# D times x on GpSimd in the chunk loop of a state-space stage, and finished chunks turned one step later

## The reference, cut to what matters

```
x = silu(conv(xbc)); xs, bm, cm = split(x)            # xs: 8 heads of 64
y_f, fin_f = ssd_chunked(xs, dt_f, a_f, bm, cm, init_f)
y_b, fin_b = ssd_chunked(flip(xs), flip(dt_b), a_b, flip(bm), flip(cm), init_b)
y = y_f + flip(y_b) + d_skip[:, None] * xs
y = y * silu(z)
out = rms_norm(y, g_out)
```

## Time and profile before

| | us |
|---|---|
| median of 3 runs | 1674.86 (1671.91 to 1675.18) |
| the profiled execution | 1675.81 |
| its span, first to last instruction | 1673.9 |
| TensorE busy | 1625.1 (97%) |
| VectorE busy | 1018.1 (61%) |
| ScalarE busy | 705.4 (42%) |
| GpSimd busy | 101.5 (6%) |

### The profile page before, as it was taken

The page is one execution under the profiler, slowest core; times in us unless marked ns, Lnnn a source line. Parts: engine busy times, 40 slices in busy tenths (PEclk is TensorE's granted clock), DMA queues, the critical chain, the costliest instruction groups (busy, mean ns, idle before and its releaser), DMA issues. The chain is left out here.

```text
span 1673.9 us, 25018 instructions
## 1 busy us (share of the span) xinstructions
PE 1625.1 (97%) x9735; PEld 1416.4 (85%) x9735; DVE 1018.1 (61%) x1689; ACT 705.4 (42%) x1288; POOL 101.5 (6%) x123
## 2 busy tenths in 40 slices
PE   6999999999899999999999999999999999999997
PEld 4787888877688889878889999999999998888886
DVE  3653645258754555555587666656665665477787
ACT  4632112357554544545664333333333334434453
POOL 1101000013000000321000000000000000000011
PEclk9999999999999999999999999999999999999999
DMA  9323441013300000323312222212222226763445
GB/s 370 148 98 144 155 157 52 1 49 102 83 11 10 14 1 2 107 88 132 126 51 79 90 81 106 106 73 90 90 95 82 100 81 216 231 219 98 124 162 191
DMA packets 76293, 176.36 MB, mean 105 GB/s; under 512 B 10352, under 2 KB 26944, under 8 KB 74128
## 3 DMA queue, kind: packets, MB, share of 16 engines
q1 hardware_dynamic: 72080, 169.75, 29.1%
q0 software_dynamic: 4096, 5.01, 0.9%
HBM read 131.02 MB, written 43.70 MB: 104 GB/s over the span
## 5 line engine op out<-in xcount | busy, mean ns | idle before, releaser
L374 PE MATMUL psF<-gv,gu_ring 128*128 128x384 f32 (+1 forms) x664 | 220.7, 332 | 3.9 <-DVE gv L2745 3.2
L375 PE MATMUL psF<-gv,gu_ring 128*128 128x384 f32 (+1 forms) x664 | 220.1, 332 | 0.0
L376 PE MATMUL psF<-gv,gu_ring 128*128 128x384 f32 (+1 forms) x664 | 220.0, 331 | 0.0
L381 PE MATMUL psF<-gv,gu_ring 128*128 128x512 f32 x540 | 193.6, 392 | 0.0
L382 PE MATMUL psF<-gv,gu_ring 128*128 128x256 f32 x540 | 151.3, 280 | 0.0
L374 PE MATMUL psF<-d_w_ring,d_hid_ring 128*128 128x512 f32 x360 | 140.2, 389 | 0.0
L375 PE MATMUL psF<-d_w_ring,d_hid_ring 128*128 128x512 f32 x360 | 140.1, 389 | 0.0
L376 PE MATMUL psF<-d_w_ring,d_hid_ring 128*128 128x512 f32 x360 | 140.1, 389 | 0.0
L374 PEld LDWEIGHTS psF<-gv,gu_ring 128*128 128x128 f32 x664 | 125.2, 189 | 10.4 <-issue 3.6
L374 PE MATMUL psP<-hT_hi,win_hi 128*128 128x512 f32 (+1 forms) x336 | 124.0, 369 | 1.8 <-DVEq L1085 1.5
L375 PEld LDWEIGHTS psF<-gv,gu_ring 128*128 128x128 f32 x664 | 125.6, 189 | 0.0
(11 more groups left out here) (457 smaller groups left out, 3710.6 us busy)
## 6 DMA issues: line engine op xcount, KB each, us to landing
hid_variants<-hraw SPq DMA_DIRECT2D x77, 320.0 KB, 2.2
d_hid<-hid_variants SPq DMA_DIRECT2D x58, 320.0 KB, 3.0
m_wring<-in_w_mod SPq DMA_DIRECT2D x16, 1024.0 KB, 4.9
d_b<-in_w_down SPq DMA_DIRECT2D x44, 256.0 KB, 4.7
win_raw<-in_w_in SPq DMA_DIRECT2D x18, 512.0 KB, 5.7
w_mod_staged<-in_w_mod SPq DMA_DIRECT2D x16, 512.0 KB, 15.2
d_hid_more<-hid_variants SPq DMA_DIRECT2D x19, 320.0 KB, 3.2
raw_gu<-in_w_gate SPq DMA_DIRECT2D x11, 512.0 KB, 3.9
```

What stands on the lines that cost most here:

```text
L374: pe.matmul(out, w_hi, x_hi, start=first, stop=False, skip_group_check=onto)
L375: pe.matmul(out, w_hi, x_lo, start=False, stop=False, skip_group_check=onto)
L376: return pe.matmul(out, w_lo, x_hi, start=False, stop=last, skip_group_check=onto)
L381: pe.matmul(both, w_hi, x_both, start=first, stop=False, skip_group_check=onto)
```

## The change

**D times x.** TensorE's four products with `ddiag` go, and with them `ddiag` and its four ScalarE copies; the weighted sum now starts the bank itself. Instead GpSimd loads `d_skip` (128x8), and in the sweep, behind ScalarE's copy of x of a chunk, multiplies `xs(c)` by it and writes the product over the chunk's columns of `xbcT`, which nothing reads any more (`xd(c)`). In the chunk loop a new `carried(c)` on GpSimd, behind `decay(c)` and ahead of `rstd(c - 1)`, adds `xd(c)` to `off_b` and then `off_b` to `yv`. VectorE's sum L1164 goes; ahead of the sum with `A[3]` it waits for `y_summed` instead.

**Turning.** TensorE's `y_turn(c - 2)` stands where `y_turn(c - 1)` stood; the last chunks are turned at the end, chunk 7 ahead of the last weighted sum. On ScalarE the order behind the exponents is now `weigh(c + 1)`, `mix(c - 2)`, `scale(c - 1)`. The square writes its unused result to a buffer of its own (`sq_junk`).

```diff
-        ddiag = at("ddiag", "conv_acc", 2048, [P, 4, P])
+        sq_junk = at("y_sq_junk", "conv_acc", 2048, [P, SW])
+        dskip = at("d_skip", "conv_acc", 4608, [P, SH])[:]
...
+        xd = lambda c: L.xbcT[:, 0:4, chunk(c)]
...
+            pool.dma_start(dskip, L.dram["d_skip"].to_broadcast([P, SH])).then_inc(d_loaded, 16)
...
+            pool.wait_ge(d_loaded, 16)
+            for i, c in enumerate(down):
+                pool.wait_ge(x_copied, 2 * i + 1)
+                p.mark(pool.tensor_tensor(heads4(xd(c)), heads4(xs(c)), per_head(dskip), ALU.mult))
+            p.wait()
+
+            def carried(c):
+
+                pool.wait_ge(off_b_read, c + 1)
+                p.link(pool.tensor_tensor(quads(off_b[:]), quads(off_b[:]), xd(c), ALU.add))
+                pool.wait_ge(off_f_read, c + 1)
+                pool.tensor_tensor(yv[:, c % 2, :], yv[:, c % 2, :], off_b[:], ALU.add).then_inc(y_summed, 1)
+
             pool.wait_ge(s_ready, NS)
             for c in range(NT):
                 decay(c)
+                carried(c)
...
-                elif i == 6:
-                    for a in range(4):
-                        act.activation(ddiag[:, a, :], L.ident, ACT.Copy, scale=dskip[:, a:a + 1]).then_inc(consts, 1)
...
                 act.wait_ge(y_ready, c + 1)
                 if c >= 1:
-                    act.wait_ge(y_turned, c)
-                act.activation(yn[:], yv[:, c % 2, :], ACT.Square, accum_out=ss[:, c:c + 1]).then_inc(squared, 1)
+                    act.wait_ge(squared, c)
+                act.activation(sq_junk[:], yv[:, c % 2, :], ACT.Square, accum_out=ss[:, c:c + 1]).then_inc(squared, 1)
...
+                if c >= 1:
+                    act.wait_ge(y_turned, c)
...
                     exponents(c + 1)
+                    weigh(c + 1)
+                if c >= 2:
+                    mix(c - 2)
                 if c >= 1:
                     scale(c - 1)
-                    mix(c - 1)
-                if c + 1 < NT:
-                    weigh(c + 1)
+            mix(NT - 2)
...
-                dve.wait_ge(off_f_read, c + 1)
-                dve.wait_ge(off_b_read, c + 1)
-                f.link(dve.tensor_tensor(yv[:, c % 2, :], yv[:, c % 2, :], off_b[:], ALU.add))
-
                 if c + 1 < NT:
                     next_state(c)
                     weights_in_chunk(c + 1)
 
+                dve.wait_ge(y_summed, c + 1)
                 dve.wait_ge(diag_done, c + 1)
...
-                if c >= 3:
-                    pe.wait_ge(mix_ready, c - 2)
+                if c >= 4:
+                    pe.wait_ge(mix_ready, c - 3)
...
+                if c == NT - 1:
+                    pe.wait_ge(cb_read, NT)
+                    pe.wait_ge(mix_ready, NT - 3)
+                    y_turn(NT - 3)
...
-                for a in range(4):
-                    pe.matmul(A[3][:, chunk(a)], L.xbcT[:, a, chunk(c)], ddiag[:, a, :], start=(a == 0), stop=False)
                 pe.wait_ge(w_ready, c + 1)
...
-                if c >= 1:
-                    if c + 1 < NT:
-                        pe.wait_ge(cb_read, c + 2)
-                    if c >= 2:
-                        pe.wait_ge(mix_ready, c - 1)
-                    y_turn(c - 1)
+                if 2 <= c < NT - 1:
+                    pe.wait_ge(cb_read, c + 2)
+                    if c >= 3:
+                        pe.wait_ge(mix_ready, c - 2)
+                    y_turn(c - 2)
+            pe.wait_ge(mix_ready, NT - 2)
+            y_turn(NT - 2)
```

More of the change, by code:

```diff
@@ L69 @@
 MOD_ALL = 6 * D // MOD_W
-C_GPRE, C_GFFN, C_BMOD, C_GQ, C_GKV, C_CW, C_CB, C_GS, C_DB, C_AL, C_DS = 0, 8, 16, 64, 67, 69, 93, 101, 105, 121, 137
-N_COLS = 141
+C_GPRE, C_GFFN, C_BMOD, C_GQ, C_GKV, C_CW, C_CB, C_GS, C_DB, C_AL = 0, 8, 16, 64, 67, 69, 93, 101, 105, 121
+N_COLS = 137
 K_ID, K_MASK, K_SEL, K_FOLD, K_TRI, K_SA, K_SB, K_MT, K_MD, K_SUM, K_SUM4 = 0, 128, 384, 400, 528, 656, 672, 672, 688, 704, 706
@@ L488, in phase_front @@
          s_ready, cb_done, cb_read, seg_done, exp_done, off_done, off_f_read, off_b_read, w_ready, diag_done, y_ready, squared,
-         rstd_ready, yn_ready, y_turned, mix_ready, sf_ready, dec_ready, fin_mm, fin_cp, consts, pch) = (
+         rstd_ready, yn_ready, y_turned, mix_ready, sf_ready, dec_ready, fin_mm, fin_cp, consts, pch, y_summed) = (
              L.sem("ss_" + n) for n in (
@@ L1398, in y_turn @@
                 mm.then_inc(y_turned, 1)
-            pe.wait_ge(consts, 9)
+            pe.wait_ge(consts, 5)
             pe.wait_ge(ones_set, 1)
@@ L1445, in _ @@
                         mm = pe.matmul(A[3][rows, h * SP_:(h + 1) * SP_], wt[:, c % 2, h, rows],
-                                       xs(c)[:, h // 2, (h % 2) * SP_:(h % 2 + 1) * SP_], start=False, stop=(h == SH - 1))
+                                       xs(c)[:, h // 2, (h % 2) * SP_:(h % 2 + 1) * SP_], start=(h == 0), stop=(h == SH - 1))
                 mm.then_inc(diag_done, 1)
-                if c >= 1:
-                    if c + 1 < NT:
-                        pe.wait_ge(cb_read, c + 2)
-                    if c >= 2:
-                        pe.wait_ge(mix_ready, c - 1)
-                    y_turn(c - 1)
+                if 2 <= c < NT - 1:
[5 more added lines that the diff above has]
+            y_turn(NT - 2)
             pe.wait_ge(off_f_read, NT)
@@ L3395 @@
             col(a["g_ssm_out"][0]), np.tile(a["dt_bias"].reshape(1, 16), (P, 1)),
-            np.tile(a["a_log"].reshape(1, 16), (P, 1)),
-            np.repeat(a["d_skip"][0].reshape(4, 2).T, P // 2, axis=0)], axis=1),
-        "b_mod": a["b_mod"], "g_post_mix": a["g_post_mix"], "g_post_ffn": a["g_post_ffn"],
+            np.tile(a["a_log"].reshape(1, 16), (P, 1))], axis=1),
+        "d_skip": a["d_skip"], "b_mod": a["b_mod"], "g_post_mix": a["g_post_mix"], "g_post_ffn": a["g_post_ffn"],
         "w_mod": w_mod.reshape(KD, P, MOD_ALL, MOD_W).transpose(2, 1, 0, 3).reshape(MOD_ALL, P, KD * MOD_W), "w_in": np.stack([k_tiles(in_tile(*e)) for e in TILES] + z_tiles),
```

4 lines of the change are left out of this document (2 added, 2 removed).

## The result

| | before | after |
|---|---|---|
| median, us | 1673.38 (4 runs, 1670.45 to 1675.18) | 1697.36 (4 runs, 1694.44 to 1699.45) |
| span of the profiled execution, us | 1673.9 | 1697.1 |
| mean granted clock of TensorE | 0.993 | 0.984 |
| GpSimd busy, us | 101.5 | 142.4 |

The change makes the kernel slower: ratio 1.0147, 95% interval 1.0133 to 1.0162, some 24 us. The forecast was 1679.1 (+4.2) with a range of 1672 to 1685. The sign was right, the size was not, and the time lies outside the range.

The account below looks back on a forecast made before the run. TensorE was taken as the bound. Eight chunk periods +1.0, first chunk +0.8, last chunk +2.4, later turning and sweep 0: +4.2 us, so 1679.1 us on the median, range 1672 to 1685.

Parts of the forecast that it names:

- part 3: Chunk loop: GpSimd's sums take turns with VectorE's weights operations; period 7.50 against 7.38 us, +1.0 us over eight periods.
- Rival (c): Chunk loop: TensorE's clock falls with gaps of 1.1 us per chunk; +10 to +16, 1685 to 1691 us; chance 0.07.
- Parts 1 and 2: Chunk loop: four products leave TensorE, one sum leaves VectorE; chunk takes 6.4 to 6.6 us, saving 0.8 to 0.9.
- Part 4: First chunk: the second sum meets chunk 1's weights operation ahead of the first gate product; +0.8 us.
- Part 5: Last chunk: no weights operations follow to hide the sums, so norm, scale, store and attention come later; +2.4 us.
- Part 6: Chunks turned one step later: TensorE holds as many transposes and the norm gets room; where it hides, nothing.
- Part 7: Sweep: GpSimd's product D times x delays VectorE's weighing of x, with 0.1 us to spare for TensorE; nothing.
- Rival (a): Chunk loop: the sums find gaps in VectorE's row and the saving comes; -4.0 us, 1671 us; chance 0.15.

Follow-up runs that it names:

- e1: Changed kernel with load_u(c + 2) issued behind the decay and ahead of GpSimd's two sums; 1681.6 us, ratio 1.0055.
- e3: Changed kernel, load left behind the norm, GpSimd's two sums replaced by memsets that read nothing (output incomplete); 1692.0 us, ratio 1.0122.
- e2: e1 with GpSimd's two sums replaced by memsets that read nothing (output incomplete); 1671.0 us, ratio 0.9999.
- e8: Changed kernel with GpSimd's two sums left out and nothing in their place (output incomplete), load behind the norm; 1671.3 us, ratio 1.0000.
- e9: e8 with SyncE's three attention loads for chunk 8 moved into the attention's block; 1667.3 us, ratio 0.9971.
- e11: Kernel before with SyncE's three attention loads for chunk 8 moved into the attention's block; 1671.5 us, ratio 1.0005.
- e5: Kernel before with only the later turning, its ScalarE order and the square's own buffer; 1673.6 us, ratio 1.0012.
- e7: Kernel before with four memsets that nobody reads on GpSimd ahead of each load_u; 1677.9 us, ratio 1.0032.
- e6: Kernel before with later turning; GpSimd makes D times x in the sweep as two bf16 tiles, TensorE adds them by the identity; 1676.9 us, ratio 1.0030.
- e12: e10 with turning, ScalarE order and the square's result as in the kernel before; 1671.5 us, ratio 0.9998.
- e4: e1 with the second sum (off_b and yv) given back to VectorE behind the weights operations; 1677.7 us, ratio 1.0027.
- e10: e6 with TensorE's wait for GpSimd's last product moved to its first use, and SyncE's loads as in e9; 1670.1 us, ratio 0.9976.

## Why the prediction was wrong

**The step that failed is part 3, where it says "By its length alone it fits".** It counted GpSimd's work per chunk, 4.34 us, "the issue of one load and the hand-overs", against the period, and went on to the norm as the only thing behind the sums. The load itself was not followed: who waits for it, and when. `carried` stands ahead of it in GpSimd's list, so it is issued behind both sums and behind the norm that queues behind L1140. The prediction had its start: the norm ends 4.17 us behind L1137's start, and L1137 stands 3.42 us behind the decay, so 7.6 us after the decay's start, where in the kernel before it was 2.23. With 2.9 us to land and TensorE's need 6.60 us behind the decay in the kernel before (386.78 - 380.18), that is a wait of some 4 us. Measured: one wait of 1.27 us and then four of 3.7 to 4.4, these in every second chunk, since the slow work behind each leaves the next load time enough. The load's place is worth 16 us between the changed kernel and e1, 21 between e3 and e2. Even with the load first the kernel is some 9 to 10 us slower than the one before, and not 4: the rest of the forecast was too low too, by the loop (part 3) and by the end (parts 5 and 6).

**Rival (c), the clock.** Named, given 0.07, and priced at 1685 to 1691. Its mechanism is what happened, but its cause was not the 1.1 us of part 3: with gaps of about 1.04 us in nearly every chunk, and one of 1.99, e1's clock is 1.00 in the whole loop. The cause was the load. That about half of a chunk's work would run at half speed was near (6 us at 0.50, four times); the price, at most +16, was too low because it went with gaps of 1.1 us and not of 4.

**Parts 1 and 2, the shorter loops: right, but not to be had.** e8 and e9 have periods of 6.53 us where nothing is late (6.4 to 6.6 was said). But TensorE then wants `pick` 3.4 us behind its issue, some loads take longer, and the mean period is 7.0 in e8 and 6.8 in e9.

**Part 3, the collisions: the mechanism right, the period 0.3 us too short.** The operations measure 1.27 us for a sum and 1.04 for the product, as taken. L1154, L1157 and the second sum stretch in turn, most to 1.8 to 2.3 us. In e1, worked back from the ends as in the prediction, L1157 really begins 2.20 us behind L1154 (377.57 against 375.37; 2.22 was said), and L1175 4.99 behind it (4.92). From L1175 to the next L1154 it is 2.81 instead of 2.58, 0.18 of that the hand-over from L1167 to L1154, 0.21 where the prediction took 0.03. So with the load out of the way the period is 7.83 instead of 7.50. That the prediction had 7.8 for whole lengths exclusive is chance: the 0.15 us of overlap is there (the sum ends at 377.72). The Trainium skill, page "SBUF — State Buffer", section "Who interferes with whom", says that a VectorE operation with two SBUF inputs contends with a GpSimd operation that reads SBUF and not with one that only writes it. The runs agree: e2's memsets are 0.52 to 0.55 us long and its weights 1.23, beside each other, and e1's sums cost 1.1 us per chunk.

**Part 4, the first chunk: right.** It can be read from the first sums of decays on. In the kernel before, where they start at 349.05, the loop's first products stand here:

```profile
355.65 1.13 PE L1428 MATMUL psP<-sf,xbcT 128*128 128x256 f32 x4 [1.56 <-DVEq L1129]
```

From the first sums of decays to these, the carried parts of chunk 0, it is 6.60 us in the kernel before, where the clock fell, and 4.96 in the changed one (348.23 to 353.19); to the first gate product it is 15.82 (364.87) and 15.09 (363.32). Without the 1.64 us of the clock that is 15.09 against 14.18, and 14.18 it is in e11 too, where the clock stayed: +0.9, +0.8 was said.

**Part 5, the last chunk: right in its chain.** In e1 L1175 of chunk 9 starts at 426.81 and L1185 at 430.81, 4.0 us (4.1 said):

```profile
430.81 0.69 DVE L1185 TENSOR_TENSOR yv<-yv,m_psC 128x512 f32<-128x512 f32 x1 [2.71 <-POOL yv L717]
```

But +2.4 us for the end was too little: it is +3.4 in e1 and +4.1 in the changed kernel, and hardly for the sums, since without them (e8) it is already +3.2. The clock has fallen there too (in e1 after TensorE had stood 4.07 us at the transposes of chunk 8, so that the last transposes and state products ran at 1.2 GHz), and SyncE's row is nearly as long as the engines' work: without any sum, but turned later, the end is 12.57 (e5).

**Part 6, the later turning: wrong.** "Where it hides, nothing" looked at TensorE, ScalarE and the norm, and not at SyncE's row, past which each finished chunk also goes. Alone it lengthens the end by 2.9 us (e5), and costs 0.12%.

**Part 7, the sweep: right.** The product stretches VectorE's weighing of x there to 1.4 us, and TensorE never waits for it.

**Rival (a)** could not have come with this change as it stands: even without the two sums (e8) the ratio is 1.0000.

## What to carry to other kernels

Work that is put ahead of a transfer's issue moves the transfer by all of it, with what queues in front of the operations between; so for every step put into an engine's list, write down what is behind it, who waits for each, and when. The same goes for the queue that stores results: a step moved one pass later puts one pass more behind the loop's end. And a saving on the engine that is the bound makes every operand due sooner: a transfer that had 1.5 us to spare at its median length has 0.5 in e8, and its longer ones are waited for.

## What the runs showed of the hardware

- TensorE's granted clock stayed at 1.00 in the loop behind waits of 0.5 to 1.2 us (e1, e7, e8), also when one of about 1.04 us came in nearly every chunk, and behind single ones of 1.55 (e3) and 1.99 us (e1). Behind one of 2.19 us (e3) and all of 3.5 to 4.4 us in the loop (after, e3) it was at 0.50, the lower level, and the fp32 matmul of 66x512 took 0.98 us instead of 0.58.
- The gap of 1.72 us ahead of the chunk loop is in all these kernels but e6, where it is 4.22 (in e7 it is 1.75). Behind it the clock fell in seven profiled executions (before, e2, e3, e5, e8, e9, e12) and not in six (after, e1, e4, e7, e10, e11). From the first sums of decays to the carried parts of chunk 0 it is 6.6 us where it fell and 4.96 where it did not, so the fall costs 1.6 us. The place of the gap itself differs by up to 1.6 us between profiles (first sums of decays at 347.62 in e10 and 349.26 in e7). Two profiles of kernels that differ by 2 us are to be compared behind that place.
- GpSimd's operations on 128x1 take their turn with VectorE's too: L693 took 0.19 us alone and 1.04 behind a weights operation, L694 0.55 and 1.55.
- The 16 KB transfer of `load_u` took 2.4 to 4.4 us from issue to landing within one kernel (e8), median 2.9.
